# Rows of narrow products in front of TensorE's waits, the modulations' sums at other steps, and the Fourier stage reordered

## The reference, cut to what matters

```python
for l in range(DEPTH):
    x = x + FFN_HALF * swiglu(rms_norm(x, ffn1_norm[l]), ffn1_w_gate_up[l], ffn1_w_down[l])
    u = rms_norm(x, mix_norm[l]) @ w_in[l]
    # ssd_mixer, mlstm_mixer and rwkv7_mixer, each on its part of u
    x = x + jnp.concatenate([y_ssd, y_ml, y_rw], axis=-1) @ w_out[l]
    x = x + FFN_HALF * swiglu(rms_norm(x, ffn2_norm[l]), ffn2_w_gate_up[l], ffn2_w_down[l])
```

## Time and profile before

| | us |
|---|---|
| median of 3 runs | 3461.74 (3459.65 to 3469.56) |
| the profiled execution's own time | 3463.73 |
| its span, first to last instruction | 3461.7 |
| TensorE busy / DVE busy / ACT busy | 3247.6 / 2101.1 / 1308.7 |
| granted TensorE clock, mean over the span | 0.972 |

### The profile page before, as it was taken

The page is one execution under the profiler, slowest core; times in us unless marked ns, Lnnn a source line. Parts: engine busy times, 40 slices in busy tenths (PEclk is TensorE's granted clock), DMA queues, the critical chain, the costliest instruction groups (busy, mean ns, idle before and its releaser), DMA issues.

```text
span 3461.7 us, 45970 instructions
## 1 busy us (share of the span) xinstructions
PE 3247.6 (94%) x19010; PEld 2824.2 (82%) x19010; DVE 2101.1 (61%) x2545; ACT 1308.7 (38%) x1584; POOL 115.8 (3%) x126
## 2 busy tenths in 40 slices
PE   7998988999998898899999999999999999999998
PEld 7978877898988786798788877788878888787797
DVE  6757557776866657677775754775343333544654
ACT  4434244444435234543421233422233122444443
POOL 0001200000000210000000000000000000000000
PEclk9999999999999998999999999999999999999999
DMA  6542022555553112455443531343222222323452
GB/s 250 230 152 86 27 95 77 200 235 204 211 207 104 38 60 72 177 208 211 153 164 123 183 124 37 122 165 122 91 85 98 91 98 80 118 98 109 164 183 98
DMA packets 83835, 462.96 MB, mean 134 GB/s; under 512 B 7573, under 2 KB 11285, under 8 KB 43562
## 3 DMA queue, kind: packets, MB, share of 16 engines
q1 hardware_dynamic: 77952, 451.45, 35.6%
q10 hardware_dynamic: 5674, 8.57, 0.8%
HBM read 458.95 MB, written 1.05 MB: 133 GB/s over the span
## 4 chain that ended last, share of the span: by engine, by line
PE 64%; DVE 25%; ACT 7%; issue 2%; DMA 0%; ACTq 0%; POOL 0%; DVEq 0%; POOLq 0%
PE ps L100 64%; DVE lo L311 8%; DVE acc L459 5%; ACT hi L305 3%; PE ps L546 1%; DVE acc L456 0%; DVE m0restMs L1980 0%; DVEq L86 0%; DVE xt L701 0%; DVE f11rot L875 0%; DVE f10rot L875 0%; DVE f20rot L875 0%; ACT f20hf_h L853 0%; ACT f11hf_h L853 0%; ACT f10hf_h L853 0%
## 5 line engine op out<-in xcount | busy, mean ns | idle before, releaser
L311 DVE TENSOR_TENSOR lo<-raw,hi 128x2048 fp32r<-128x2048 f32 (+1 forms) x357 | 809.6, 2268 | 622.8 <-ACT hi L305 601.5
L305 ACT ACTIVATE hi<-raw 128x2048 fp32r<-128x2048 f32 (+1 forms) x357 | 676.1, 1894 | 572.7 <-PE ps L100 541.9
L459 DVE SCALAR_TENSOR_TENSOR acc<-raw,sil,acc 128x512 f32<-128x512 f32 x504 | 379.0, 752 | 20.7 <-DVE f21hf_l L877 0.5
L100 PE MATMUL ps<-half00hs,hi 128*128 128x512 f32 x672 | 209.3, 393 | 0.6 <-DVE lo L311 0.6
L100 PE MATMUL ps<-half02hs,hi 128*128 128x512 f32 x672 | 209.0, 392 | 0.7 <-DVE lo L311 0.7
L100 PE MATMUL ps<-half10hs,hi 128*128 128x512 f32 x672 | 208.7, 392 | 0.8 <-DVE lo L311 0.7
L100 PEld LDWEIGHTS ps<-half10hs,hi 128*128 128x128 f32 x672 | 125.7, 188 | 28.5 <-DVE lo L311 1.6
L100 PEld LDWEIGHTS ps<-half02hs,hi 128*128 128x128 f32 x672 | 125.4, 188 | 27.6 <-DVE lo L311 1.1
L100 PEld LDWEIGHTS ps<-half00hs,hi 128*128 128x128 f32 x672 | 125.2, 188 | 27.3 <-DVE lo L311 1.0
L100 PE MATMUL ps<-half10hs,lo 128*128 128x512 f32 x352 | 137.6, 391 | 0.0
L100 PE MATMUL ps<-half02hs,lo 128*128 128x512 f32 x352 | 137.6, 391 | 0.0
(11 more groups left out here) (919 smaller groups left out, 7900.3 us busy)
## 6 DMA issues: line engine op xcount, KB each, us to landing
raw<-in_ffn_w_gate_up SPq DMA_DIRECT2D x88, 1024.0 KB, 9.0
raw<-in_ffn_gu SPq DMA_DIRECT2D x88, 1024.0 KB, 5.0
raw<-in_ffn_w_down SPq DMA_DIRECT2D x85, 1024.0 KB, 5.2
raw<-in_ada_w SPq DMA_DIRECT2D x72, 1024.0 KB, 5.1
raw<-in_w_in_t SPq DMA_DIRECT2D x28, 1024.0 KB, 5.0
raw<-in_ret_w_in SPq DMA_DIRECT2D x24, 1024.0 KB, 4.9
raw<-in_w_out SPq DMA_DIRECT2D x16, 1024.0 KB, 5.0
raw<-in_w_in_n SPq DMA_DIRECT2D x12, 1024.0 KB, 5.0
```

The source lines that it names most:

```text
L100: return p().matmul(o, l, r, start=start, stop=stop, skip_group_check=True)
L305: a().activation(self.high(w), self.raw[self.place(r)][:, 0:width], ACT.Copy).then_inc(*a.mark(self.wac, w))
L311: v().tensor_tensor(self.low(w), self.raw[self.place(r)][:, 0:width], self.high(w).bitcast(F32), ALU.subtract).then_inc(*v.mark(self.wdv, w))
L459: v().scalar_tensor_tensor(out=acc[:, n, :], in0=w[:, k, :], scalar=s, in1=acc[:, n, :], op0=ALU.mult, op1=ALU.add).then_inc(*v.mark(self. ...
```

## The change

1. `K.idle(p, bank, n)` issues n products of `ones` (128x128) by the first mask (the identity), 128 columns wide, in float32 into a bank that nobody reads then. Such rows stand directly in front of waits: in every norm but the first (15 for f20, f11, f21; 14 for mn0, mn1; 30, 17, 22, 22 for half00, half02, half10, ret; 21 for half12), in `ProjRw` 12, `Prep` 6, `Inv` 16 twice, `Scan` 16, `Rest` 7, `Ssd` 7, 22 and 12, each in both layers, in `Ret`'s last head 10, in `Out` 20. Four row tiles' norms first wait for the first row of the stage before; `Ssd` has two added waits (`xt`, 3 and `across`, 0).
2. `soon` is gone: f21 is filled behind two of three gate/up steps. Single down groups are filled when their number is even.
3. Fourier: the split of `wx` moves ahead by one step (behind the first half's products with `d1`). The weight tiles wait for `lo, 1, q` instead of `lo, 1, 4`, the banks' evictions and the gates are waited for where they are first needed, and `lo, 1, 4` in front of the last products. Two of the Gates' phases come earlier in the list.

```diff
@@ -295,6 +295,11 @@
+    def idle(self, p, bank, n):
...
+        for _ in range(n):
+            mm(p, self.ps[bank][:, 0:128], self.ones, self.msk[:, 0, :])
@@ -504,6 +509,8 @@
+    idle = None
@@ -535,6 +542,10 @@
         K.ada.clear(p)
+        if self.idle:
+            if len(self.rows) == 4 and not self.turn[0]:
+                self.before[0].row(p, 0, 1)
+            K.idle(p, *self.idle)
         p.wait_ge(*self.dv["xs", self.turn[-1]])
@@ -1040,6 +1051,8 @@
                 p.wait_ge(*self.dv["us", 2 * q - 7])
+            if q == 2:
+                self.K.idle(p, 2, 12)
             project_t(self, p, self.M.hx, self.norm, q, q, self.K.ps[q % 4])
@@ -1108,6 +1121,7 @@
         yield
+        K.idle(p, 7, 6)
         p.wait_ge(*A["sq"])
@@ -1313,6 +1327,7 @@
             x.then_inc(*p.mark(E, "bv", T))
+            K.idle(p, 1, 16)
             p.wait_ge(*D["bv", T])
@@ -1500,6 +1515,7 @@
         Yc = M.Yc.rearrange("p (t h) n -> p t (h n)", t=2)
+        K.idle(p, 0, 16)
         p.wait_ge(*D["Yn", 1])
@@ -1618,6 +1634,8 @@
         for q in range(7):
+            if q == 3:
+                K.idle(p, 7, 7)
             wh, wl = (w.rearrange("p (k n) -> p k n", k=8) for w in self.ready(p, q))
@@ -1803,6 +1821,7 @@
             if n == 3:
+                K.idle(p, 4, 7)
                 p.wait_ge(*D["en"])
@@ -1824,6 +1843,9 @@
         for n in range(10):
+            if n == 0:
+                p.wait_ge(*A["xt", 3])
+                K.idle(p, 0, 22)
             if n < 6:
@@ -1838,6 +1860,8 @@
         yield
+        p.wait_ge(*D["across", 0])
+        K.idle(p, 1, 12)
         p.wait_ge(*D["yn", 3])
@@ -2386,6 +2410,8 @@
                 j = 2 * n + chunk
+                if j == 0 and t == 0:
+                    K.idle(p, 0, 20)
                 p.wait_ge(*self.dv["ys", j // 4])
@@ -2512,17 +2538,22 @@
                     yield
-        p.wait_ge(*self.dv["lo", 1, 4])
-        self.finish.gates.done(p)
         for q in range(4):
...
                 j, c = 2 * q + jj, slice(t * 128, (t + 1) * 128)
+                p.wait_ge(*self.dv["lo", 1, q])
+                if at < 4 and q == 0:
+                    for n in ((), (37, 38), (39, 40), (41,))[t]:
+                        p.wait_ge(*self.dv["e", n])
+                    if t == 3:
+                        self.finish.gates.done(p)
                 for h in range(2):
...
                     if j == 7:
+                        p.wait_ge(*self.dv["lo", 1, 4])
                         x = mm3(p, b[:, :], *(f[0:5, c] for f in self.fx), *(w[0:5, ns] for w in self.wxs), False, True)
@@ -2566,13 +2597,13 @@
                     if g == 4:
-                        if s == 0:
-                            a.wait_ge(*self.second.all)
-                            a().activation(self.wxs[0][0:5, :], self.wx[0:5, :], ACT.Copy).then_inc(*a.mark(A, "wx"))
                         a.wait_ge(*self.dv["e", n])
...
                     self.squares(a, 1)
+                elif (s, i) == (0, 15):
+                    a.wait_ge(*self.second.all)
+                    a().activation(self.wxs[0][0:5, :], self.wx[0:5, :], ACT.Copy).then_inc(*a.mark(A, "wx"))
                 if i in (7, 15, 20):
@@ -2628,10 +2659,6 @@
                         self.low(v, s, 3)
-                        if s == 0:
-                            v.wait_ge(*self.ac["wx"])
-                            v().tensor_tensor(self.wxs[1][0:5, :], self.wx[0:5, :], self.wxs[0][0:5, :].bitcast(F32),
-                                              ALU.subtract).then_inc(*v.mark(D, "wx"))
                         v.wait_ge(*self.ac["hi", s, 4])
@@ -2640,6 +2667,9 @@
                     self.norm_dve(v, 1)
+                    v.wait_ge(*self.ac["wx"])
+                    v().tensor_tensor(self.wxs[1][0:5, :], self.wx[0:5, :], self.wxs[0][0:5, :].bitcast(F32),
+                                      ALU.subtract).then_inc(*v.mark(D, "wx"))
                     yield
@@ -2779,6 +2809,8 @@
                 self.project(p, h + 1, 1)
+            if h == 3:
+                K.idle(p, 0, 10)
             p.wait_ge(*D["yn", h, 1])
@@ -2918,7 +2950,7 @@
-    def ffn(s, gates=(), soon=False, late=0):
+    def ffn(s, gates=(), late=0):
@@ -2926,7 +2958,7 @@
                     fill(2)
-                elif j % (4 if soon else 3) < (3 if soon else 2):
+                elif j % 3 < 2:
                     fill()
@@ -2934,7 +2966,7 @@
                         run(s)
-                    if s.nt == 2 and g[0] % 3 == 0:
+                    if s.nt == 2 and g[0] % 2 == 0:
                         fill()
@@ -2962,6 +2994,7 @@
         s.since = since
+        norm.idle = None if before is setup else (0, 15) if which == 1 else (4, 15)
         if before is setup:
@@ -2976,6 +3009,7 @@
                                   K.at(ROWS + 8192, f"mn{l}no", 3, 512), lambda c, s: K.col(l, "nm", c)))
+        norm.idle = 0, 14
         prw = put(f"prw{l}", ProjRw(K, l, M, norm))
@@ -3077,7 +3111,8 @@
                                  (ROWS, 50176), 16384, [2, 3, 0, 1])
-    ffn(s, [norm, norm], soon=True, late=8)
+    norm.idle = 0, 30
+    ffn(s, [norm, norm], late=8)
     fill_to(18)
@@ -3085,19 +3120,21 @@
     four = put("four", Fourier(K, "four", half, 0, both, Gated(gates, both, rot)))
-    for s in (half, half, four, half, half, four, four, gates, four, four, gates, four, gates, four, gates, four, gates):
+    for s in (half, half, four, half, half, four, gates, four, gates, four, four, four, gates, four, gates, four, gates):
         run(s)
...
                                  90112)
+    norm.idle = 0, 17
     join(four, norm)
...
                                  (45056, 67584), 69632)
+    norm.idle = 0, 22
     join(before, norm)
@@ -3123,6 +3161,7 @@
     half.since = [ret]
+    norm.idle = 0, 21
     join(rout, norm)
```

## The result

The changed kernel took 3443.72 us (median of 4 runs, 3442.49 to 3445.3) against 3460.87 us for the kernel before on the same chip (4 runs): ratio 0.9946, 95% interval 0.9934 to 0.9958. It is faster, by 17 us where 36 were forecast, and lies outside the range of 3409 to 3440. The profiled execution has a span of 3442.6 us, 19.1 us less than before.

A forecast was written before the change was run, and what follows sets the result against it. TensorE, busy 94%, was taken as the bound, through its idle and low-clock time. 7.3 + 10.0 + 3.6 + 1.1 + 11.9 + 1.9 + 2.2, less 1.4 and 0.3, gave 36.3 us: 3425 as median, range 3409 to 3440.

The forecast's parts named there:

- rival 1: All rows: they do not hold the clock and the low stretches stay; 3447 us, chance 0.10.
- rival 4: All 30 rows run at the low level, 0.43 us a product, and delay what follows; 3538 us, chance 0.03.
- The norms' term: Norms and the turns behind yn: transposes start at the high clock, 9 x 0.4 = 3.6 us gained.
- the Fourier stage: Transforms: work moved ahead of the second half's transposes gains 1.9 us, weight tiles waiting only for their own lo 2.2.
- `Ret`/`Out`: Behind the stage's entry: 20 products overrun, but 13 wide products then run at the high clock; gain 1.1 us.
- Sum 7.3: Mixer of layer 0: clock regained in low stretches behind ProjRw, bv (twice) and Yn, 7.3 us.
- Sum 10.0: Mixer of layer 1: clock regained behind ProjRw, bv, Yn and in the second part, 10.0 us.
- rival 2: Low stretches leave, but slack takes half of the mixers' 17.3 us and others come at uncovered waits; 3437 us, chance 0.15.
- rival 3: More leaves: low stretches at 448, 1260, 2158 and 2090 us, and the transforms' upper bound; 3414 us, chance 0.15.
- Sums of f21, 11.9: f21: filling two of three gate/up steps removes the acc waits and low stretches behind them, 11.9 us gained.
- What moves, minus 1.4: Down-group fills and loads move, otherwise hidden; half02's clear may wait for DVE's bias, 1.4 us lost.

The follow-up runs named there:

- e12_norows: The changed kernel with idle() empty, so without any row, its waits, sums and Fourier order kept: 3455.92 us (0.9983).
- e2_sums: The kernel before with the modulations' sums at the new steps alone, added waits kept but no row products: 3459.16 us (0.9990).
- e3_four: The kernel before with the Fourier stage's new order alone: 3460.69 us (0.9997).
- e10_clear: The changed kernel with 5 products in front of half00's first down product (half02's row was missing): 3444.14 us (0.9950).
- e18_weak: e16_weak timed and profiled once more: 3431.03 us (0.9918).
- e16_weak: e15_best with 6 full-width products behind the block of 64-row, 64-column products at the end of Inv in each mixer: 3433.58 us (0.9919).
- e15_best: The changed kernel with three more rows a mixer, 9 products in Rest, and 5 before the first down products of half00 and half02: 3434.41 us (0.9920).

## Why the prediction was wrong

**What was right.** The rows hold the clock: without them its mean in the profile is 0.977 instead of 0.989 and 12 us are lost, so rival 1 falls. Of rival 4's cold rows there were few: in the second profile of the changed kernel `Ssd`'s row in front of `yn` lies in a low stretch in both layers (from 556 and 1369 us) and takes 4.3 us for its 12 products instead of 2.9. Mean clock 0.989, norm waits filled and the transposes at the high level came as their steps say. The norms' term (2.8 without the turns, about 3 measured by taking their rows away) and the Fourier stage fit in size but aren't clear of the scatter: the part between the first transposes of the stage and of half02 is 4.7 us shorter in the first profile and 3.3 in the second, forecast 1.9 + 2.2 and a norm's 0.4. `Ret`/`Out` came out by luck: the part is 1.0 us shorter, forecast 1.1, but it is 1.0 shorter without any row too (`e12_norows`) and 1.4 in `e2_sums`, so no run shows that the rows there bring it.

**The step that failed** is the clock terms of the mixers, "Sum 7.3" and "Sum 10.0". I took every low stretch of the one trace before that lies on TensorE's chain, found a row in front of it, and gave back all of it. Measured by taking the inner rows away, they are worth 9.8 us; in the first profile the mixers became 1.2 and 5.4 us shorter, 10.7 less than 17.3. The booked stretches did go. But others came up on TensorE's chain. In the two mixers the chain held 62 us of TensorE inside low stretches before and holds 47 and 49 in the two profiles of the changed kernel; times 0.46 that is 7.1 and 6.1 us, beside mixers that became 6.6 and 7.9 us shorter. Of the 47, ten stretches of 3.4 us are new, an estimated 15.5 us lost again: four behind the grown waits (320, 573, 1133, 1385 us), two 3 us behind the wait of 1.2 us for the reciprocal in `Prep` (293, 1106), and four in the scan behind no such wait (471, 477, 1283, 1297). The first two points below are about these; the third is a place that my sum left out, before and after alike.

1. *What TensorE gained in front of a wait for VectorE came back in the wait, and the clock fell behind it.* The wait at the entry of `Inv` grew to 3.2 us and `MixOut`'s to 3.6, a growth of 7.7 us over both layers, with low stretches behind both in both layers. Rows there removed these, and the kernel gained 3.8 us (intervals overlapping, so the size isn't shown). This is rival 2, which I gave 0.15 and a price of 12 us. It named its two uncovered waits wrongly, though (`ml` and 1.7 us in front of the outputs), and covering `ml` alone brought nothing.
2. *A low stretch of one trace is a sample.* I read layer 1's 0.88 against layer 0's 0.96 in the earlier trace rows as a property of the layer and booked 2.5 us of it. The same instructions gave the opposite order of the layers in `e3_four`. Over the four profiles whose mixers have no rows (before, `e2_sums`, `e3_four`, `e12_norows`) the two mixers sum to 797.3, 798.2, 796.0 and 795.5 us; in the two of the changed kernel to 790.7 and 789.4. The means differ by 6.7 us. The four new stretches in the scan are of this kind: the second profile doesn't have them, and has others.
3. *A low stretch without a wait ahead of it stayed.* I had seen the stretches at 448 and 1260 us and set them aside as part of rival 3, something that might leave by itself. They were booked at nothing and are in both kernels, so they are no part of the shortfall. They follow a block of 64-row, 64-column products that has 24-column products on both sides, and no row in front of a wait touches them. With six full-width products behind the block both mixers of one profile were at 389.3 us, the figure that was forecast; those of the other were at 388.2 and 394.1. In these four mixers one had no low stretch there, two had one of 3.4 us, one had two; in the 34 without them the mean is 6.6 us. The products cost 1.4 us of TensorE themselves, and the timed runs don't resolve what is left (3433.6 and 3431.0 against 3434.4). What brings the low level there is not settled (above).

**Mis-sized terms.** *Sums of f21, 11.9*: no `acc` wait is left, as forecast, but four waits of 1.0 to 2.0 us for weight splits are, and the part is 9.8 us shorter (9.2 in the kernel with the sums alone). *What moves, minus 1.4*: I priced half02's `clear` and nothing else. f20's part is 1.4 us longer (forecast 0.4 shorter), half00's 1.7 (forecast 0.4 shorter), half02's 1.3 (forecast 1.0); the waits for `mods` that end at 1795 and 2299 us have a low stretch of 3.4 us behind them, an estimated 1.6 us each. In the kernel before the wait in half00 was just as long and had none behind it. The sums alone therefore gained 3.1 us, not 11.9 less 1.4. In the first profile the shortfalls, 10.7 in the mixers, 2.1 in f21, 1.8, 2.1 and 0.3 here, make 17 us: the profiled span lost 19.1 where 36.3 were forecast.

Behind the waits of 1.4 us for `mods` the clock fell to 1.2 GHz in both profiles of the changed kernel, and a row in half00 (`e10_clear`) took the stretch there away, while the one in half02, which got no row, stayed (2297.1 us). The Trainium skill (TensorE: Matmul & The Clock Gate, the summary table) speaks of gaps of about 3 us and more; these runs don't agree. A wait of this length doesn't always bring it: the same one at 2002.76 us of the kernel before, 1.4 us, has no low stretch behind it.

**The chances.** The result lies between rival 2 (3437) and rival 1 (3447). The range reached only to 3440 because the mixers' terms were taken as bounded below by half their size, and the sums' term as exact.

**A version that beats both** is `e18_weak` (with `e16_weak` 10 runs, 3429.4 to 3440.1): 0.9918, 28 to 31 us below the kernel before beside it and, by the ratios, 9 to 11 below the changed one. `e15_best`, without the six products, can't be told from it (0.9920).

## What to carry to other kernels

Read low-clock stretches as a sample: profile the same kernel twice, and book only what TensorE's own chain holds in them on average. When work is taken out in front of a wait on another engine, that wait grows, so cover the next waits too, and try the covers together, since one alone may show nothing. The low clock can also come with TensorE busy throughout: list the forms of the products around such a place, all of them, before naming one as the cause. And don't mix single wide products into a block of small ones; put them behind it.

## What the runs showed of the hardware

- The clock fell to 1.2 GHz 1.4 to 4.7 us behind the start of a block of 48 64-row, 64-column products that TensorE ran without a gap, in 34 of 34 mixers; 24-column products, 0.11 us apart, stand on both sides of it. In and behind 64 products of the same shape between 512-column ones the clock stayed at 1.00, in 40 of 40 mixers.
- The same instructions got the low level or not from one execution to the next: the wide products at 471 us of the changed kernel started every 0.43 us in one profile and every 0.23 us in the other.
- A wait of 1.4 us had 3.4 us at 1.2 GHz behind it in one kernel (1795 us, changed) and none in another (2002.76 us, before).
- Products of 64 rows and columns overlap in a block of their own (49 start in 1.71 us). With twelve full-width instructions mixed in, two at a time, block and products took 6.09 us; with the same twelve behind it 3.07 us. Each change of form cost an estimated 0.25 us (3.02 us over twelve changes).
- Four products (0.9 us) more a row cost nearly their full length in the ten rows outside the mixers, and 1.1 to 2.4 us in all over the twenty inside.
